# A hybrid attention encoder on one core: down-projection banks, two norm matmuls and three pieces of ScalarE's queue in another order

## What is computed

```python
h = rms_norm(x, g_attn) * (1.0 + scale_a) + shift_a
proj = h @ w_in                       # q, k, v of group A; latents of group B
o_a = block_attention(q_a, k_a, v_a)  # 8 query heads, 2 key/value heads
o_b = block_attention(q_full, k_full, v_b)   # 8 heads from the latents
o = concatenate([rms_norm(o_a, g_out_a), rms_norm(o_b, g_out_b)]) @ w_o
x = x + gate_a * o

h = rms_norm(x, g_ffn) * (1.0 + scale_f) + shift_f
u = depthwise_conv_centred(h @ w_up, conv_w, conv_b)   # width 3 over tokens
val, gate = split(u, 2)
y = (silu(gate) * val) @ w_down
x = x + gate_f * y
```

## Time and profile before

| | |
|---|---|
| runs (3) | 1169.24 us median, 1169.02 to 1169.82 |
| profiled execution | 1169.24 us, span 1167.5 us |
| mean granted TensorE clock | 0.991 |
| busy, DVE / ACT / POOL | 65% / 43% / 51% |
| DMA | 151.68 MB, mean 130 GB/s |

### The profile page before, as it was taken

One profiled execution on the slowest core, in us unless ns is written; L12 is line 12 of the kernel. 1 busy time (PEld: TensorE's weight loads), 2 busy tenths in 40 slices (PEclk: granted clock), 3 DMA queues, 4 the chain that ended last, 5 costly groups with the idle time before them and its releaser, 6 DMA issues.

```text
span 1167.5 us, 18737 instructions
## 1 busy us (share of the span) xinstructions
PE 1138.8 (98%) x6264; PEld 953.0 (82%) x6264; DVE 759.3 (65%) x1466; ACT 507.7 (43%) x922; POOL 591.9 (51%) x783
## 2 busy tenths in 40 slices
PE   9999999899999999999899999999999999999996
PEld 6897677898888888888789966799888888888886
DVE  6787676767767877788667687746775144412445
ACT  5445765254422344233454567535442244323442
POOL 2483342555555545546766324255555555554552
PEclk7999999999999999999999999999999999999999
DMA  9843610424445444544433111022432322223212
GB/s 345 331 167 123 217 74 19 146 90 162 162 149 208 156 172 180 198 180 173 152 115 120 61 67 37 19 74 90 161 128 93 106 90 99 99 91 107 91 72 73
DMA packets 44123, 151.68 MB, mean 130 GB/s; under 512 B 5138, under 2 KB 7954, under 8 KB 44052
## 3 DMA queue, kind: packets, MB, share of 16 engines
q1 hardware_dynamic: 44052, 150.77, 36.1%
HBM read 148.65 MB, written 2.10 MB: 129 GB/s over the span
## 4 chain that ended last, share of the span: by engine, by line
issue 37%; POOL 29%; PE 19%; POOLq 14%; DMA 1%; DVE 0%; ACT 0%; SPq 0%; DVEq 0%; ACTq 0%
POOL w_lo L601 28%; POOLq L603 10%; PE ps L688 6%; PE ps L694 6%; PE ps L689 6%; POOLq L661 2%; POOLq L659 1%; DMA shift<-shift_slots 1%; POOLq L614 0%; PE ps L820 0%; DVE x L1657 0%; POOLq L599 0%; POOLq L604 0%; ACT w_hi L1244 0%; POOL cg_sg L632 0%
## 5 line engine op out<-in xcount | busy, mean ns | idle before, releaser
L601 POOL TENSOR_TENSOR w_lo<-w_raw,w_hi 128x256 fp32r<-128x256 f32 x712 | 551.9, 806 | 455.2 <-ACT w_hi L1244 436.0
L688 PE MATMUL ps<-h_hi,w_hi 128*128 128x512 f32 (+1 forms) x864 | 316.6, 366 | 2.1 <-POOLq L604 1.9
L689 PE MATMUL ps<-h_lo,w_hi 128*128 128x512 f32 (+1 forms) x864 | 316.0, 366 | 0.0
L694 PE MATMUL ps<-h_hi,w_lo 128*128 128x512 f32 (+1 forms) x864 | 315.9, 366 | 0.0
L1244 ACT CAST w_hi<-w_raw 128x1024 fp32r<-128x1024 f32 x178 | 185.7, 1047 | 196.5 <-PE ps L688 195.9
L2008 DVE SCALAR_TENSOR_TENSOR u_sb<-ps,par,u_sb 128x510 f32<-128x510 f32 x176 | 131.8, 749 | 99.2 <-ACT u_sb L1449 84.9
L688 PEld LDWEIGHTS ps<-h_hi,w_hi 128*128 128x128 f32 x864 | 163.3, 189 | 28.8 <-POOLq L604 2.8
L689 PEld LDWEIGHTS ps<-h_lo,w_hi 128*128 128x128 f32 x864 | 163.3, 189 | 26.2
L694 PEld LDWEIGHTS ps<-h_hi,w_lo 128*128 128x128 f32 x864 | 163.2, 189 | 26.1
L688 PE MATMUL ps<-a_hi,w_hi 128*128 128x512 f32 (+1 forms) x400 | 146.0, 365 | 4.2 <-DVE a_lo L2021 3.0
L689 PE MATMUL ps<-a_lo,w_hi 128*128 128x512 f32 (+1 forms) x400 | 145.4, 363 | 0.0
(11 more groups left out here) (181 smaller groups left out, 1504.8 us busy)
## 6 DMA issues: line engine op xcount, KB each, us to landing
w_raw<-w_slots SPq DMA_DIRECT2D x178, 512.0 KB, 3.5
ada_raw<-ada_slots SPq DMA_DIRECT2D x88, 512.0 KB, 4.1
shift<-shift_slots SPq DMA_DIRECT2D x8, 512.0 KB, 13.8
x_tok<-x_rows SPq DMA_DIRECT2D x4, 512.0 KB, 9.8
x<-x_t SPq DMA_DIRECT2D x4, 512.0 KB, 14.4
y_t<-x SPq DMA_DIRECT2D x3, 512.0 KB, 2.9
y_t<-x SPq DMA_DIRECT2D x1, 256.0 KB, 3.0
y_t<-x SPq DMA_DIRECT2D x2, 128.0 KB, 2.7
```

Of the source, the lines that this page charges most:

```text
L601: nc.gpsimd.tensor_tensor(w_lo[:, j, c], w_raw[:, j, c], w_hi[:, j, c].bitcast(F32), ALU.subtract)
L688: hh = mm(out, stat[0], mov[0], start=first, stop=False)
L689: hl = mm(out, stat[0], mov[1], start=False, stop=False)
L694: return mm(out, stat[1], mov[0], start=False, stop=last)
```

## The change

Four edits, with no instruction added or taken away.

1. The table of banks goes; output tile m of a down stage uses bank 4 + m % 2. Only tile 2 differs: bank 4 in place of bank 0.
2. In layer 1's input projection the sums stand behind k = 2 in place of k = 4, and the roots behind k = 4 in place of k = 5.
3. In round 12 ACT copies the transposes first and makes the group root second.
4. In the up loop ACT makes the odd copy behind `a_hi`, straight ahead of the even copy.

```diff
@@ -237,7 +237,7 @@
             take(("up", g, i, 0), 2 * (i % 2))
             take(("up", g, i, 1), 2 * (i % 2) + 1)
         for m in range(KD if g < len(GROUPS) - 1 else TAIL):
-            take(("down", g, m), DOWN_BANKS[m])
+            take(("down", g, m), 4 + m % 2)
     for i in range(N_UPD - TAIL):
         take(("down_half", i), HALF_BANKS[i % 3])
     return use
@@ -245,7 +245,6 @@
 
 
 HALF_BANKS = (4, 5, 2)
-DOWN_BANKS = (4, 5, 0, 5, 4, 5, 4, 5)
 KEY_BANKS = (7, 4, 5, 7)
 USES = [0] * 8
 USE = [plan_banks(L, USES) for L in range(DEPTH)]
@@ -862,9 +861,9 @@
                                         int(t == 2 * s and (k == 0 if s == 0 else k % 2 == 0 and k > 0)))
                             if k == KD - 1:
                                 last.then_inc(full[bank(key)], 1)
+                        if L > 0 and s == 0 and k == 2:
+                            norm_sums(2 * L, 1)
                         if L > 0 and s == 0 and k == 4:
-                            norm_sums(2 * L, 1)
-                        if L > 0 and s == 0 and k == 5:
                             norm_roots(2 * L, 1)
                 for k in range(KD):
                     if k % 2 == 0:
@@ -1402,10 +1401,10 @@
                 for i in range(NP + 2):
                     if i == 0:
                         take_values(2)
+                    if i >= 2:
+                        take_transposes(i - 2)
                     if i == NA + 4:
                         group_roots(L, 0)
-                    if i >= 2:
-                        take_transposes(i - 2)
                     if i < NP:
                         act.wait_ge(max_ready, NP * L + i + 1)
                         for c in range(4):
@@ -1449,14 +1448,13 @@
                                 A(u_sb[:, e, half, :], ps[:, bank(key), :], ACT.Identity,
                                   bias=par[:, L, bass.ds(ft + PC_CB, 1)],
                                   scale=par[:, L, bass.ds(ft + (PC_CW + 2 * FT), 1)]).then_inc(mid_tap, 1)
-                            n0 = L * SLOTS + S_UP[g] + 5 + 2 * e
-                            hi_slot(n0 % RING, RING * it + n0, 16 * it + 16 * (n0 // RING + 1))
                             act.wait_ge(taps_done, 2 * it + (tile + 1))
                             A(sil[:, e, :], u_sb[:, e, 1, :], ACT.Silu).then_inc(sil_ready, 1)
                             act.wait_ge(af_ready, 2 * it + (tile + 1))
                             nc.scalar.copy(a_hi[:, bass.ds(2 * it + e, 1), :], af[:, e:e + 1, :]).then_inc(a_hi_ready, 1)
-                            n0 = L * SLOTS + S_UP[g] + 6 + 2 * e
-                            hi_slot(n0 % RING, RING * it + n0, 16 * it + 16 * (n0 // RING + 1))
+                            for half in range(2):
+                                n0 = L * SLOTS + S_UP[g] + 5 + 2 * e + half
+                                hi_slot(n0 % RING, RING * it + n0, 16 * it + 16 * (n0 // RING + 1))
                     if g < len(GROUPS) - 1:
                         with act.Fori(0, KD // 4) as it:
                             for e in range(4):
```

## The result

| | before | after |
|---|---|---|
| beside each other, first time (4 runs each) | 1169.53 us (1169.02 to 1169.93) | 1182.09 us (1181.81 to 1183.28) |
| again (12 and 5 runs) | 1169.74 us (1168.51 to 1172.87) | 1181.96 us (1178.86 to 1182.76) |
| ratio, first and again, 95% interval | | 1.0113 (1.0096 to 1.0131); 1.0095 (1.0080 to 1.0110) |
| profiled execution, its span | 1169.24, 1167.5 us | 1182.05, 1180.1 us |

The account below looks back on a forecast made before the run. PE, busy 1138.8 of 1167.5 us, was taken as the bound, so added waits count in full unless covered. Terms 4.8 + 1.7 + 1.5 + 1.85 = 9.85 us on 1169.24 gave 1179.1 us; own range 1177.5 to 1180.5, wider range 1175.8 to 1182.6.

Parts of the forecast that it names:

- group root, twice: Attention round 12, both layers: the root behind the copy starts PE 0.75 us later each, 1.5 us in all.
- bank, two first groups and layer 1's second: Down stages, tile 2: PE waits for DVE to empty bank 4, 0.6 us at each of three.
- bank, layer 0's second group: Second down stage, tile 2: DVE is still in `w_ada` products, so bank 4 comes late; PE loses 3.0 us.
- bank and copies, two third down stages: Before tile 7: later odd copies delay the splits by 1.1 us in layer 0, 0.75 in layer 1; sum 1.85.
- sums and roots: Start of layer 1: PE waits for DVE's last addition to `ssum`, roots come no earlier; 1.7 us.
- the third down stages' bank wait is absorbed: Tile 2 of both third down stages: the bank's 0.6 us goes into tile 7's split wait, costing nothing.
- The stall goes into the 2.99: net 0: Layer 0, third group: the 2.7 us stall at slot 7 is absorbed by PE's later 2.99 us `a_lo` wait.
- a rival at 0.25: TensorE's clock falls in a new stall: 1180.8 us behind the 3.0 us stall, 1182.3 with the 2.7 too; chance 0.25.
- slot 7's wait: Layer 0, third group, second tile: the odd split ends at 542.36, PE asks at 539.83 and stands 2.7 us.
- layer 0's waits are paid out of the 2.99: Rival: the `a_lo` wait absorbs all PE lost before, up to 2.99 us: 1176.1 us; chance 0.12.
- PE isn't the bound: Rival: DVE's chain sets each group's end, where `a_lo` is asked for; not slower, 1169.2 us; chance 0.04.
- The splits come late more often: Rival: first tiles' spare 0.7 us fails or third group's third tile is late too: 1183 us; chance 0.08.

Follow-up runs that it names:

- the stall filled: Kernel after plus unused products of ones: 6 before tile 2 of layer 0's second down stage, 12 before slot 7 of its third group: 1178.49 us against before's 1170.19.
- the moved `w_ada` slot: Kernel before with the new bank rule; in layer 0's second group one DVE `w_ada` slot moved behind the down stage's last output tile: 1177.22 us against 1169.74.
- one moved out: Kernel before with one `w_ada` slot of layer 0's third group moved from behind up-stage tile 4 to behind the last tile: 1166.19 us against 1170.19.

## Why the prediction was off, step by step

Steps of the trace of after over before, in us; they add up to 12.5, the difference of the two spans (12.6) but for rounding.

| place | forecast | trace |
|---|---|---|
| first 40 us | 0 | +1.65 |
| group root, twice | 1.5 | +0.61, +0.61 |
| layer 0's output projection | 0 | -1.24 |
| bank, two first groups and layer 1's second | 3 x 0.6 | +0.69, +0.66, +0.70 |
| bank, layer 0's second group | 3.0 | +2.24 |
| half clock behind it | 0 | +1.72 |
| slot 7, less the `a_lo` wait | 2.7 - 2.7 | +3.79 - 3.23 |
| half clock behind slot 7 | 0 | +2.93 |
| bank and copies, two third down stages | 1.85 | +0.69 - 0.70, +0.69 - 0.71 |
| sums and roots | 1.7 | +1.42 |

**Right.** By the steps in the table, PE bounds the kernel, and a new wait counts in full unless another wait behind it hangs on something else. The bank's price where DVE is idle (0.6, measured 0.57 to 0.7), and where it is in its products (3.0, measured 3.0 alone and 2.2 in company). The wait at the sums, and that the roots don't come earlier in exchange. The group root. That one single split would be late, and which. That the third down stages' bank wait is absorbed (+0.69, then -0.70).

**Wrong: "The stall goes into the 2.99: net 0".** This is the step that failed. In after the stall, its half clock and what the `a_lo` wait gives back come to 3.79 + 2.93 - 3.23 = 3.5 us. Two things were wrong in it. First, the stall brought the clock down. With it comes the fall behind tile 2's wait (1.72 us), which the forecast also put at nothing; together the two are 4.65 us of half clock. Second, the cover was smaller than it looked. With the stall filled and the clock up, 3.78 us went in and only 2.50 came back, although 0.49 of the wait was still there, because the last `a_lo` itself came 1.4 us later. DVE did not notice the stall, as I had said; it was late by two slow instructions of its own (0.95 us, below) and by 0.5 on the way behind them.

I had the falls as a rival at 0.25, but ranked it behind the forecast because the clock had stayed up in one wait of 2.99 us. One wait in one trace was no ground for that. At this same `a_lo` wait the clock stayed up in four traces (2.94 to 2.99 us) and fell in three (2.99, 3.01 and 4.50). Elsewhere it fell behind waits of 1.69, 2.05, 2.08, 2.81, 3.61 and 3.63 us, and stayed up behind others of 1.69, 1.70 and 2.05. That the rival's 1182.3 lies so near the 1182.1 measured is luck: it has 3.2 us for the two falls (4.65 at their places, 2.7 when the waits behind them are counted in) and 1.85 for the third down stages (nothing measured), and the measured time has 1.65 us of the start in it.

**Mis-sized: slot 7's wait, 2.7 for 3.6.** I let the even copy and its split start with the tile's chain as in before. The chain itself runs 1.0 us later against PE. DVE's two small instructions before it met POOL's splits, which now come together behind `a_hi`. In after, and in before:

```profile
531.01 0.71 DVE L1557 TENSOR_SCALAR mod<-mod 128x16 f32<-128x16 f32 x1
531.79 0.62 DVE L1559 TENSOR_TENSOR mod<-mod,par 128x16 f32<-128x16 f32 x1
```

```profile
525.37 0.18 DVE L1559 TENSOR_SCALAR mod<-mod 128x16 f32<-128x16 f32 x1
525.62 0.18 DVE L1561 TENSOR_TENSOR mod<-mod,par 128x16 f32<-128x16 f32 x1
```

That is 0.97 us. In the trace of edit 4 alone they take 0.72 and 0.61, in that of edit 1 alone 0.18 and 0.17, and with the odd copies back at their old place (the third group alone) 0.17 and 0.18. What they have in common when they are slow is that a split is running as they start (in after POOL splits from 530.96 on), and not the copies as such: with edit 1 and the moved `w_ada` slot, no copy is moved, yet they start beside a split and take 0.72 and 0.62. No run took the split away by itself.

**Mis-sized: the third down stages, 1.85 for 0.** Alone the copies cost 1.04 there. In company the bank's wait (0.7) moves PE back and the splits of slots 3 to 7 fall otherwise beside DVE: one of 2.83 us stands where 3.32 stood, and PE reaches tile 7 after the last split. It hangs on little: with the stalls filled that split takes 3.31 us, and PE waits 0.97 us before tile 7 in layer 0. I had added the terms of one place by hand where only their order in time decides.

**Left out: the start, 1.65 us, and the old fall in layer 0's output projection, -1.24.** The start isn't the change's, as far as the traces tell, and the medians contain it. Of the old fall the prediction said only that it may move and go; it moved.

The rivals "layer 0's waits are paid out of the 2.99" and "PE isn't the bound" fell: with edit 1 alone the `a_lo` wait is still 3.01 us behind 4.9 us of lost time. "The splits come late more often" fell too: in after only slot 7 waits longer than before.

## What to carry to other kernels

Price a new wait on TensorE twice, at its own length and with a stretch at half clock behind it (here 1.7 us for a short stretch and 2.9 for a long one), and count a cover behind it only once; if the wait can't be avoided, filling it with idle products may help (3.5 us by the medians in two stalls of after, nothing in the output projection of before). Before adding a bank's or a copy's delay, ask which other wait ends at the same place: only the later one is paid. Where DVE is saturated, a moved piece of its work counts almost in full: 3.2 us more of waits on DVE with a slot moved in, 2.4 us less with one moved out. Compare the traces from the first changed instruction on, not from zero, when the differences are of one or two microseconds.

## What the runs showed of the hardware

- The granted clock of PE was full (2.4 GHz) or half (1.2 GHz), and behind these waits it stayed at half for 3.4 or 6.8 us. In layer 0's output projection the fall came at 220.28 us in before, behind both waits; in after it came at 217.39, between them, so that PE did its slow products while the next split was being made anyway, and lost 1.24 us less. Windows of after:

```profile
217.00:221.00 4.00, 3.82 (x19) 3.83 (x20) 3.32 (x5) 0.83 (x2) 3.69 (x4) 0.57 0.54 181
221.00:225.00 4.00, 3.59 (x30) 3.39 (x30) 3.46 (x6) 0.42 (x1) 0.73 (x1) 1.00 0.70 241
```

- Which of two equal waits brings the clock down differed from trace to trace (1.69 us fell and stayed up, so did 2.05 and 2.99). I could not tell it from the wait's length.
- The program's start has two forms, 3.0 to 3.4 us apart in eight matmuls. 60 us in, PE stands 0.4 us early to 1.1 us late against before in the traces with the short form, and 1.6 to 4.0 us late in those with the long one.
- Of the short DVE instructions on `mod` (128x16 numbers), all 65 in the thirteen traces that started while a POOL split ran took 0.50 to 0.72 us, and the 117 others 0.17 or 0.18.
